# A mixer and SwiGLU layer on one core: square roots by logarithm and exponential, sigmoids by tanh, and new distances between the chain steps

## The reference, cut to what matters

```python
def rms_norm(x, w):
    y = xf * lax.rsqrt(jnp.mean(xf * xf, axis=-1, keepdims=True) + EPS)
def l2_normalize(x):
    return xf * lax.rsqrt(jnp.sum(xf * xf, axis=-1, keepdims=True) + EPS)
def delta_inputs(p, conv_w, a_log, dt_bias):
    qkv = jax.nn.silu(depthwise_conv(p[..., :V_END], conv_w))
    q, k, v = l2_normalize(split_heads(q)), l2_normalize(split_heads(k)), split_heads(v)
    beta = jax.nn.sigmoid(ba[:, :, :2])
    g = -jnp.exp(a_log) * jax.nn.softplus(ba[:, :, 2:] + dt_bias)
def delta_output(o, z, norm_w):
    y = rms_norm(o, norm_w) * jax.nn.silu(split_heads(z))
def conformer_branch(p_glu, dw, ln_w, ln_b, n_rows):
    u = a * jax.nn.sigmoid(gate)
    u = depthwise_conv(u, dw)
    return jax.nn.silu(layer_norm(u, ln_w, ln_b))
x = x + g1 * rms_norm(mix @ w_out, mix_norm_post)
x = x + g2 * rms_norm(swiglu(modulate(rms_norm(x, ffn_norm_pre), sh2, sc2), ...), ffn_norm_post)
```

## Time and profile before

| | |
|---|---|
| median of 3 runs | 1626.45 us (1623.65, 1626.45, 1626.49) |
| span of the profiled execution | 1622.9 us |
| TensorE, VectorE, ScalarE, GpSimd busy | 1538.2, 1043.9, 769.2, 227.5 us |
| weights and other data read | 331.15 MB |

### The profile page before, as it was taken

The page is one execution under the profiler, slowest core; times in us unless marked ns, Lnnn a source line. Parts: engine busy times, 40 slices in busy tenths (PEclk is TensorE's granted clock), DMA queues, the critical chain, the costliest instruction groups (busy, mean ns, idle before and its releaser), DMA issues.

```text
span 1622.9 us, 25136 instructions
## 1 busy us (share of the span) xinstructions
PE 1538.2 (95%) x9297; PEld 1292.8 (80%) x9297; DVE 1043.9 (64%) x1458; ACT 769.2 (47%) x1045; POOL 227.5 (14%) x236
## 2 busy tenths in 40 slices
PE   4887999998999999999999999999999999999998
PEld 0557788887888898898877888888888888888786
DVE  1436899999896857675577544545454445777554
ACT  5536634444355745467356544444444443443432
POOL 2000223333332333244200000000000000000000
PEclk9998999999999999999999999999999999999999
DMA  9993555655564556554464666666666665998653
GB/s 353 400 378 108 180 186 194 197 178 184 173 202 134 174 199 191 174 196 134 139 231 132 207 185 192 188 188 191 185 192 194 184 191 187 334 325 319 223 187 135
DMA packets 190979, 334.59 MB, mean 206 GB/s; under 512 B 14707, under 2 KB 80355, under 8 KB 189986
## 3 DMA queue, kind: packets, MB, share of 16 engines
q1 hardware_dynamic: 190194, 330.89, 62.8%
q0 software_dynamic: 688, 2.39, 0.5%
HBM read 331.15 MB, written 2.10 MB: 205 GB/s over the span
## 4 chain that ended last, share of the span: by engine, by line
PE 81%; DVE 10%; DMA 2%; SPq 2%; ACT 2%; issue 2%; POOL 0%; DVEq 0%; ACTq 0%; POOLq 0%
PE PS L1848 66%; DVE cacc L1706 3%; DVE w_lo L1409 3%; DMA first<-in_w_mod_dram 2%; PE PS L1854 2%; PE PS L2117 2%; PE PS L2069 2%; PE PS L2163 2%; SPq L755 2%; DVE sil L1534 1%; PE PS L2015 1%; PE PS L1944 1%; PE PS L2059 1%; DVE xyi L1597 1%; DVE gh L1592 1%
## 5 line engine op out<-in xcount | busy, mean ns | idle before, releaser
L968 ACT ACTIVATE w_hi<-raw 128x1024 fp32r<-128x1024 f32 (+1 forms) x422 | 443.9, 1056 | 508.1 <-PE PS L1848 415.5
L1376 DVE TENSOR_TENSOR w_lo<-raw,w_hi 128x1024 fp32r<-128x1024 f32 x264 | 323.0, 1225 | 309.6 <-ACT w_hi L968 309.6
L1848 PE MATMUL PS<-w_hi,h_hi 128*128 128x512 f32 x704 | 275.7, 392 | 0.0
L1848 PE MATMUL PS<-w_hi,h_lo 128*128 128x512 f32 x704 | 274.6, 390 | 0.0
L1848 PE MATMUL PS<-w_lo,h_hi 128*128 128x512 f32 x704 | 274.4, 390 | 0.0
L1848 PE MATMUL PS<-h_hi,w_hi 128*128 128x256 f32 (+1 forms) x784 | 237.4, 303 | 0.0
L1409 DVE TENSOR_TENSOR w_lo<-raw,w_hi 128x1024 fp32r<-128x1024 f32 (+1 forms) x158 | 195.5, 1249 | 57.6 <-ACT w_hi L968 57.6
L1848 PE MATMUL PS<-h_hi,w_lo 128*128 128x256 f32 (+1 forms) x784 | 221.8, 283 | 0.0
L1848 PE MATMUL PS<-h_lo,w_hi 128*128 128x256 f32 (+1 forms) x784 | 221.6, 283 | 0.0
L1848 PEld LDWEIGHTS PS<-h_hi,w_hi 128*128 128x128 f32 (+1 forms) x784 | 148.5, 189 | 36.8 <-issue 30.2
L1848 PEld LDWEIGHTS PS<-w_hi,h_lo 128*128 128x128 f32 x704 | 132.4, 188 | 27.7
(11 more groups left out here) (342 smaller groups left out, 2352.8 us busy)
## 6 DMA issues: line engine op xcount, KB each, us to landing
raw<-in_w_in_dram SPq DMA_DIRECT2D x128, 512.0 KB, 3.9
raw<-in_w_mod_dram SPq DMA_DIRECT2D x96, 512.0 KB, 4.9
raw<-in_w_gate_dram SPq DMA_DIRECT2D x88, 512.0 KB, 3.7
raw<-in_w_up_dram SPq DMA_DIRECT2D x88, 512.0 KB, 3.7
raw<-in_w_down_dram SPq DMA_DIRECT2D x88, 512.0 KB, 4.5
first<-in_w_mod_dram SPq DMA_DIRECT2D x64, 512.0 KB, 9.7
raw<-in_w_out_dram SPq DMA_DIRECT2D x32, 512.0 KB, 4.3
gin<-in_w_mod_dram SPq DMA_DIRECT2D x32, 512.0 KB, 5.9
```

The lines of the kernel that those rows point to most:

```text
L968: act.activation(out_ap, in_ap, ACT.Copy).then_inc(S[kind], 1)
L1376: dve.tensor_tensor(w_lo[:, slot, :], raw[:, (R0 + n) % RING, :], w_hi[:, slot, :].bitcast(F32), ALU.subtract).then_inc(S["lo"], 1)
L1848: ins = pe.matmul(out_ap, a[i], b[j], start=start and n == 0, stop=stop and n == 2, skip_group_check=grouped)
```

## The change

Two table sets are named, and ScalarE's code loads one when the next function isn't in the one loaded: one has exponential and logarithm, the other SiLU and tanh. 1/sqrt(x) becomes exp(-0.5 * ln(x)), both on ScalarE; all of VectorE's reciprocals go. A sigmoid becomes 0.5 * tanh(x / 2) + 0.5: for beta with one more VectorE instruction, for the GLU with the factor 0.5 in the convolution's weights. The table AFTER has new numbers, and each step nrc and orc moves into the group of its logarithm.

```diff
+            def using(name):
+                if table[0] != name:
+                    act.preload_act_table_set(name)
+                    table[0] = name
+            def inverse_root(out_ap, log_ap):
+                using(EXP_LN)
+                return act.activation(out_ap, log_ap, ACT.Exp, scale=-0.5)
...
-                        copy(vcol[:, VC_C31:VC_C31 + 248], PS[:, b, 0:248], kind)
+                        act.activation(vcol[:, VC_C31:VC_C31 + 248], PS[:, b, 0:248], ACT.Copy, scale=0.5).then_inc(S[kind], 1)
...
+                elif kind == "nrc":
+                    need(act, "nrt", *key)
+                    a = 8 if key[1] == "k" else 12
+                    inverse_root(rstd[:, a:a + 4], rtmp[:, a:a + 4]).then_inc(S[kind], 1)
+                elif kind == "lnr":
+                    need(act, "lsd")
+                    inverse_root(cx[:, 0, :], cx[:, 1, :]).then_inc(S[kind], 1)
...
                     need(act, "baT", s)
...
-                        ins = act.activation(gates_[s]["beta"][:, d, :, :], pr[:, :, 8 * d:8 * d + 8], ACT.Sigmoid)
+                        using(SILU_TANH)
+                        ins = act.activation(gates_[s]["beta"][:, d, :, :], pr[:, :, 8 * d:8 * d + 8], ACT.Tanh,
+                                             scale=0.5)
...
                     need(act, "ny", s)
                     y2 = gates_[s]["y2"][:, :, :, :]
+                    using(EXP_LN)
                     act.activation(y2, y2, ACT.Exp).then_inc(S[kind], 1)
...
                     need(act, "nsq", *key)
                     a = 8 if what == "k" else 12
-                    act.activation(rtmp[:, a:a + 4], sums[:, a:a + 4], ACT.Sqrt,
+                    using(EXP_LN)
+                    act.activation(rtmp[:, a:a + 4], sums[:, a:a + 4], ACT.Ln,
...
-                    act.activation(sgb[:, :], pr, ACT.Sigmoid).then_inc(S[kind], 1)
+                    using(SILU_TANH)
+                    act.activation(sgb[:, :], pr, ACT.Tanh, scale=0.5).then_inc(S[kind], 1)
...
+                    dve.tensor_scalar(g["beta"][:, :, :, :], g["beta"][:, :, :, :], 0.5, 0.5, ALU.mult, ALU.add)
...
-                elif kind == "nrc":
-                    need(dve, "nrt", *key)
-                    a = 8 if key[1] == "k" else 12
-                    dve.reciprocal(rstd[:, a:a + 4], rtmp[:, a:a + 4]).then_inc(done, 1)
...
-                    dve.tensor_tensor(ub[:, :], projection(dve, ("a", LAT, i)), sgb[:, :], ALU.mult).then_inc(done, 1)
+                    dve.scalar_tensor_tensor(out=ub[:, :], in0=sgb[:, :], scalar=1.0, in1=projection(dve, ("a", LAT, i)),
+                                             op0=ALU.add, op1=ALU.mult).then_inc(done, 1)
...
-         "nsq": [0, 0, 0, 0, 0, 0, 0, 0], "kn": [4, 3, 4, 6, 4, 4, 4, 3], "kT": [4, 7, 6, 4, 4, 4, 4, 4], "kk": [0, 3,
+         "kn": [4, 0, 4, 4, 4, 4, 4, 3], "kT": [4, 3, 6, 3, 4, 3, 4, 4], "kk": [0, 3, 1, 0, 0, 0, 1, 2], "kk1": [0, 0, 7, 1,
```

More of the change, by code:

```diff
@@ L1204, in _ @@
                     need(act, "osq", *key)
-                    act.activation(rtmp[:, 16:20], sums[:, 16:20], ACT.Sqrt, bias=cst[:, 0:1],
+                    using(EXP_LN)
+                    act.activation(rtmp[:, 16:20], sums[:, 16:20], ACT.Ln, bias=cst[:, 0:1],
                                    scale=1.0 / P).then_inc(S[kind], 1)
@@ L1232, in _ @@
                     need(act, "lva", 3)
-                    act.activation(cx[:, 1, :], cx[:, 0, :], ACT.Sqrt, bias=cst[:, 0:1],
+                    using(EXP_LN)
+                    act.activation(cx[:, 1, :], cx[:, 0, :], ACT.Ln, bias=cst[:, 0:1],
                                    scale=1.0 / DC).then_inc(S[kind], 1)
@@ L1330, in _ @@
                 if v == 8:
-                    act.activation(rtmp[:, 4:5], cst[:, 0:1], ACT.Sqrt, bias=cst[:, 0:1])
+                    using(EXP_LN)
+                    using(EXP_LN)
                 if v in (30, 52, 74):
@@ L1342, in _ @@
                 act.wait_ge(f_rc, t + 1)
-                act.activation(rtmp[:, t:t + 1], rtmp[:, 2 + t:3 + t], ACT.Sqrt, bias=cst[:, 0:1],
+                using(EXP_LN)
+                act.activation(rtmp[:, t:t + 1], rtmp[:, 2 + t:3 + t], ACT.Ln, bias=cst[:, 0:1],
                                scale=1.0 / D).then_inc(f_rt, 1)
+                act.wait_ge(f_rt, 2 * t + 1)
+                inverse_root(rstd[:, t:t + 1], rtmp[:, t:t + 1]).then_inc(f_rt, 1)
         @block.vector
@@ L1410, in _ @@
                                       ALU.subtract).then_inc(done, 1)
-                elif kind == "xrc":
-                    s = key[0]
-                    col = slice(4 + key[1], 5 + key[1]) if s == FFN else slice(2 * s, 2 * s + 2)
-                    need(dve, "xrt", *key)
-                    dve.reciprocal(rstd[:, col], rtmp[:, col]).then_inc(done, 1)
                 elif kind == "xdg":
@@ L1655, in _ @@
                     dve.tensor_reduce(sums[:, 16:20], kd[:, :, :], AX_X, ALU.add).then_inc(done, 1)
-                elif kind == "orc":
-                    need(dve, "ort", *key)
-                    dve.reciprocal(rstd[:, 16:20], rtmp[:, 16:20]).then_inc(done, 1)
                 elif kind == "on":
@@ L1724, in _ @@
                         dve.tensor_tensor(cx[:, 0, :], ps, cx[:, 0, :], ALU.add).then_inc(done, 1)
-                elif kind == "lnr":
-                    need(dve, "lsd")
-                    dve.reciprocal(cx[:, 0, :], cx[:, 1, :]).then_inc(done, 1)
                 elif kind == "lnn":
@@ L1752, in _ @@
                     dve.tensor_reduce(sums[:, o:o + 1], sums[:, a:a + n], AX_X, ALU.add).then_inc(done, 1)
-                elif kind == "yrc":
-                    t, = key
-                    need(dve, "yrt", t)
-                    dve.reciprocal(rstd[:, 6 + t:7 + t], rtmp[:, 6 + t:7 + t]).then_inc(done, 1)
                 elif kind == "fl":
@@ L1834, in _ @@
                 dve.tensor_tensor(anf[:, t, :], PS[:, 6 + t, :], gw_all[:, 1536:2048], ALU.mult).then_inc(f_yg, 1)
-                dve.wait_ge(f_rt, t + 1)
-                step(dve.reciprocal(rstd[:, t:t + 1], rtmp[:, t:t + 1]))
+                dve.wait_ge(f_rt, 2 * t + 2)
                 dve.wait_ge(f_yg, 7 + t)
```

68 lines of the change are left out of this document (47 added, 21 removed), and 9 rows, old and new, of the table AFTER.

## The result

| | before | changed |
|---|---|---|
| median | 1626.47 us (4 runs, 1623.65 to 1627.41) | 1616.55 us (4 runs, 1614.47 to 1617.11) |
| span of the profiled execution | 1622.9 us | 1615.3 us |
| ratio, 95% interval | | 0.9938 (0.9926 to 0.9950) |
| busy: TensorE, VectorE, ScalarE | 1538.2, 1043.9, 769.2 us | 1536.8, 1035.5, 741.2 us |

The change makes the kernel 9.9 us faster. The forecast was 4.9 us, 1621.5 us, with a range from 1616.5 to 1627.0; the median lies on the lower edge of that range.

A forecast was written before the change was run, and what follows sets the result against it. TensorE was taken as the main bound, VectorE from 226 to 400 us, ScalarE only at the first gates. Terms summed to -4.9 us: span 1622.9 to 1618.0, median 1621.5 us, range 1616.5 to 1627.0.

The forecast's parts named there:

- first gates: 144 to 157 us, ScalarE the bound: three loads gone, split 2.9 to 3.0 us earlier, TensorE gains 2.0 us.
- second gates: At 178 us: one load fewer, but the remaining two now stand behind waits; +0.1 us.
- z projection, vnew: First z, near 571 us: load behind a wait, +0.5 us; around 558 us: exponential ahead of copy vnew, +0.2 us.
- short reciprocals: Three or four keys' reciprocals leave VectorE's full queue between 226 and 540 us: -0.6 us; the others covered.
- LayerNorm's reciprocal: 128x256 on VectorE at 534.29 us, 1.74 us long, on the path to zi; its removal gains 1.7 us.
- taps at 600 us: VectorE's second taps move ahead of kd and hc_lo, the SiLU comes 3 us earlier: -1.4 us.
- other new distances: Reordered steps from 362 to 388 us, at 440 us and ahead of zi: 0, range -1.2 to +2.0 us.
- a full queue ends where it did: VectorE's full queue, 362 to 388 us: only order changes, the work's sum doesn't, so 0 us.
- slower: Rival: products e_, moved up in VectorE's full queue, block it waiting for TensorE; +10.8 us, 1632 us, chance 0.10.
- The clock pays as well: Rival: same gains, and one or both clock falls near 385 and 541 us gone; 1618 us, chance 0.14.
- Absorbed: Rival: first gates' gain given back before 226 us, taps at 600 us only trade waits; -1.5, 1625 us, chance 0.23.
- Drain: Rival: each load holds ScalarE 1.4 us beyond its row, so second gates gain 1.3 us; 1620 us, chance 0.03.

The follow-up runs named there:

- old_table: The changed kernel with the old numbers in the table AFTER (former reciprocals stay in their new groups): 1622.18 us, ratio 0.9974 to the kernel before.
- ln_recip: The changed kernel with the LayerNorm's 128x256 reciprocal put back on VectorE, its result unused: 1616.3 us, ratio 0.9947 to the kernel before.
- three_more: The changed kernel with three table loads added at the context's gates, each of the set already loaded: 1617.76 us, ratio 0.9953 to the kernel before.
- mlo_after_kn: old_c4 with GpSimd's products mlo held until VectorE has done kn: 1617.22 us, ratio 0.9941 to the kernel before.
- old_c4: The changed kernel with the old AFTER numbers for the context's fourth head pair alone: 1619.41 us, ratio 0.9960 to the kernel before.
- before_again: The kernel before, unchanged, profiled once more in a single execution: 1626.34 us.
- new_table: The kernel before with the new numbers in AFTER alone, its square roots, reciprocals and sigmoids kept: 1617.73 us, ratio 0.9949 to the kernel before.
- before_c4: The kernel before with the new AFTER numbers for the context's fourth head pair alone: 1622.4 us, ratio 0.9973.
- after_again: The changed kernel, unmodified, run once more as the yardstick: 1614.88 us, ratio 0.9936 to the kernel before.

## Why the prediction saw only half of the gain

| step | forecast | measured |
|---|---|---|
| first gates | -2.0 | -2.95 (22.60 to 19.65, in every profile) |
| second gates | +0.1 | -0.1 (before and old_table, 178-241: 62.84, 62.76) |
| z projection, vnew | +0.7 | +0.8 and +0.2 (offsets of the matmuls at 573 and 560 us, before and old_table) |
| short reciprocals | -0.6 | 0 (before and old_table, 312-432: 119.9, 119.9) |
| LayerNorm's reciprocal | -1.7 | -1.6 (ln_recip) |
| taps at 600 us | -1.4 | -0.2 to -0.4 |
| other new distances | 0 (-1.2 to +2.0) | -4 to -5 |
| load ahead of the queries' decays | not seen | +0.4 |
| sum | -4.9 | -8 or so by these rows; -8.9 behind 145 us and -7.6 in all by the first two profiles; -9.9 by the medians |

**The code's terms held, but for the gates' size.** Loads, gates, z, vnew and the large reciprocal came to -3.5 us in the forecast (with the short reciprocals) and to -4.2 us in old_table. The gates were mis-sized: I had the shift of ScalarE's split right (2.9 to 3.0 us) and then gave TensorE only the 2.0 us of its two visible waits. The column shows the whole shift arriving. The waits are listed from the modelled end of a matmul; by the starts of the matmuls they are 0.9 and 1.5 us, and the other 0.55 us of the 2.95 come in steps of up to 0.3 us between 159 and 167 us. three_more gives the same answer from the other side, 3.6 us for three loads.

**The step that failed is "a full queue ends where it did".** I put the moved instructions between 362 and 388 us at 0, since VectorE was busy for 98% there and the sum of its work doesn't change by order. Both halves were wrong. The sum did change. In the old order kn and the four instructions ahead of it took 2.1 us more because GpSimd's mlo ran beside them, and TensorE got those 2.1 us late (mlo_after_kn). In the changed kernel mlo (from 370.20 us) runs beside other products of the convolution: four of them (128x240) take 3.73 us there and 2.94 before. They stand just ahead of xyi, for which TensorE waits 1.66 us, so a part of the overlap may still be paid. From the four products 128x252 to the second xf_ctx, the same instructions but for one reciprocal of 0.17 us, VectorE takes 34.0 us before and 30.6 after; 1.9 us of that is shorter work. The other 1.4 us are waits, for the queue was not full at that place. TensorE waited for kn and twice more, then VectorE three times between 385 and 389 us, twice for TensorE (0.21 and 0.81 us) and once for ScalarE (0.41 us):

```profile
373.94 0.66 PE L1854 MATMUL PS<-ident,kn 128*128 128x128 f32 x4 [1.19 <-DVE kn L1548]
...
381.06 0.47 PE L2078 MATMUL PS<-xyi,nid_r 128*128 128x512 f32 x1 [1.43 <-issue]
...
383.70 0.50 PE L2078 MATMUL PS<-xyi,nid_r 128*128 128x512 f32 x1 [1.33 <-DVE e_ L1553]
...
388.98 0.42 DVE L1553 TENSOR_TENSOR e_<-PS,e_ 128x256 f32<-128x256 f32 x1 [0.81 <-PE PS L2024]
```

One engine's wait is handed to the other. The pair's new order has none of VectorE's three waits. I had even written down the wait for kn and its 1.56 us, and did not ask why it was 1.56 and not 0.69 as for the seven other kn of that kernel. So of the 4.2 us that this pair's order costs in old_c4, 2.1 are the overlap with GpSimd; how the rest divides between the handed-on waits and the clock, whose fall I kept for the range, no run separates, nor whether kn's place alone would do it.

**The taps at 600 us** failed by the rule that I had applied elsewhere: of a step that is delayed, every reader counts. I named kd and hc_lo as 2 us late and took them as harmless. hc_hi, ScalarE's copy of kd, stands ahead of pi in ScalarE's queue, and TensorE waits for pi.

**Rivals.** The "slower" one (VectorE blocked at e_) did not happen: its waits for level products are 47.5 us in 23 where they were 42.4 in 24, VectorE's idle time from 226 to 400 us is 6.1 us, 1.9 more than before, where 5 would have decided for it, and the stretch is shorter. "The clock pays as well" was the nearest (1618 us), for a mechanism that is half true at most: the fall at 384 us was in all five profiles with the pair's old numbers and in three of eleven with the new ones; the fall at 541 us was in the first profile of the kernel before and not in before_again, new_table, before_c4 or ln_recip, which have the same wait for zi ahead of it (1.26 to 1.46 us). By these profiles it belongs to the execution and not to the kernel. "Absorbed" fell for the gates: the 3.6 us of three_more are still there at the end (2.8 us by ratio), with its later columns as in after_again; of the taps at 600 us it was right. "Drain" fell: in the traces an activation that waits for nothing else follows its load within 0.02 us, and the three switches less at the gates gave 2.95 us, which is 3 x 1.28 less the 0.9 us that the prediction took off. (The loads of three_more reload the set in place, so they say nothing on a switch.) The Trainium skill ("ScalarE: Activation LUTs", What ACT_TABLE_LOAD costs) gives 2.66 us for every switch to a different set; an estimate from it is 8 us for three, 7.1 with the 0.9 taken off, and the measurement decides against it here.

**Two sums of the prediction don't come out.** The lower end of its range, "both falls of the clock gone and the order's -1.2", is 1621.5 - 3.4 - 1.2 = 1616.9 us, not 1616.5; the measured 1616.55 lies just below what its own terms give. And for "drain" the second gates' terms give 1.4 us less and not 1.2, which its time of 1620 us has right.

**What stays open.** The columns add up to 7.6 us between the two first profiles and the medians to 9.9 and 10.4 us. Behind the mark at 145 us the two profiles of the kernel before have 1477.9 and 1479.5 us and those of the changed kernel 1469.0 and 1468.7 us, 8.9 to 10.8 us less, as the medians say. What hides it is the first 145 us (143.7 to 147.0 us in sixteen profiles, with the kernels mixed), whose variation no experiment here explains. The column of 178 to 241 us varies with a fall of the clock near 187 us that some kernels with the new numbers have and others don't.

## What to carry to other kernels

When a queue is full, its order still counts, by who waits for each instruction on the other engines and by what runs beside it: look for one instruction that is longer than its equals, and for two engines that wait for each other in turn. A load of a function table costs next to nothing while its engine waits, and up to its whole length behind that wait or ahead of a copy that another engine wants, so put the load ahead of the waits, not merely early. To compare two traces, measure between marks of equal work: the length of a stage then mostly repeats within 0.1 us where order and clock are the same, while whole executions of one kernel differ by 3 us and more.
